# mLSTM heads for four samples at once, with the prompt's final state made in one piece ahead of the samples

## What is computed

```python
def step(carry, inp):                       # one block of frames, b and m are gate sums and running maxima
    C, n, m = carry                         # C: (512 v, 512 k) for each head and stream
    ...
    s = jnp.einsum('bhjd,bhsd->bhjs', qb, kb) * w
    num = jnp.einsum('bhjs,bhsv->bhjv', s, vb) + wp[..., None] * jnp.einsum('bhvd,bhjd->bhjv', C, qb)
    den = jnp.sum(s, axis=-1) + wp * jnp.einsum('bhd,bhjd->bhj', n, qb)
    h = num / jnp.maximum(jnp.abs(den), jnp.exp(-mj))[..., None]
    ...
    C_new = wpL[..., None, None] * C + jnp.einsum('bhs,bhsv,bhsd->bhvd', wsL, vb, kb)
    n_new = wpL[..., None] * n + jnp.einsum('bhs,bhsd->bhd', wsL, kb)
hC = _head_layernorm(hC, norm) + skip * xc  # then x = x + (hC * silu(zg)) @ w_down1
```

## Time and profile before

| | |
|---|---|
| time, median of 3 runs | 2386.26 us (2384.49 to 2390.1) |
| the profiled execution: its time / its span | 2387.82 us / 2386.0 us |
| mean granted TensorE clock | 0.968 of 2.4 GHz |
| TensorE busy / VectorE / ScalarE / GpSimd | 94% / 42% / 20% / 35% |
| bytes moved | 224.24 MB, 94 GB/s over the span |

### The profile page before, as it was taken

One profiled execution on the slowest core, in us unless ns is written; L12 is line 12 of the kernel. 1 busy time (PEld: TensorE's weight loads), 2 busy tenths in 40 slices (PEclk: granted clock), 3 DMA queues, 4 the chain that ended last, 5 costly groups with the idle time before them and its releaser, 6 DMA issues.

```text
span 2386.0 us, 35273 instructions
## 1 busy us (share of the span) xinstructions
PE 2233.5 (94%) x13637; PEld 1985.8 (83%) x13637; DVE 1008.2 (42%) x1342; ACT 474.7 (20%) x695; POOL 845.1 (35%) x492
## 2 busy tenths in 40 slices
PE   6999997899999999999999898998979899999997
PEld 5898996899999998999875564745559899999996
DVE  4565565432220025793236566474642322220025
ACT  4333333211110002221221302213110211100011
POOL 4323321545454545554401000010115454444443
PEclk9999999899999999999999899998989999999998
DMA  4121221212222222322223416062352122222222
GB/s 165 52 89 54 84 87 38 71 62 70 77 73 78 72 77 90 117 79 100 94 87 145 176 48 251 22 229 93 139 198 71 62 71 76 73 75 75 77 73 88
DMA packets 57295, 224.24 MB, mean 94 GB/s; under 512 B 6288, under 2 KB 11280, under 8 KB 48272
## 3 DMA queue, kind: packets, MB, share of 16 engines
q1 hardware_dynamic: 48576, 202.94, 24.1%
q10 hardware_dynamic: 8656, 20.39, 2.3%
HBM read 170.06 MB, written 53.25 MB: 94 GB/s over the span
## 4 chain that ended last, share of the span: by engine, by line
PE 78%; DVE 10%; issue 4%; DMA 3%; ACT 3%; DVEq 1%; POOL 0%; SPq 0%; ACTq 0%; POOLq 0%
PE psd L204 10%; PE psd L208 9%; PE psd L209 9%; PE psd L205 9%; PE psd L211 9%; PE psd L210 9%; PE psm L1217 3%; DMA Cs<-st_c 3%; DVE cv L902 2%; PE psd L1126 2%; PE psm L1188 2%; DVE ntmp L277 2%; PE psm L1224 2%; PE psd L1224 2%; PE psm L382 2%
## 5 line engine op out<-in xcount | busy, mean ns | idle before, releaser
L1722 POOL CAST whi<-wraw 128x1024 fp32r<-128x1024 f32 x224 | 238.7, 1066 | 963.9 <-PE psd L211 504.8
L1724 POOL TENSOR_TENSOR wlo<-wraw,whi 128x1024 fp32r<-128x1024 f32 x224 | 543.4, 2426 | 17.9
L204 PE MATMUL psd<-xh,whi 128*128 128x320 f32 x1280 | 407.3, 318 | 31.7 <-ACT xh L250 19.1
L208 PE MATMUL psd<-xl,whi 128*128 128x320 f32 x1280 | 402.4, 314 | 10.8 <-POOL xl L285 8.7
L205 PE MATMUL psd<-xh,whi 128*128 128x320 f32 x1280 | 399.2, 312 | 0.0
L209 PE MATMUL psd<-xl,whi 128*128 128x320 f32 x1280 | 398.7, 312 | 0.0
L210 PE MATMUL psd<-xh,wlo 128*128 128x320 f32 x1280 | 398.7, 311 | 0.0
L211 PE MATMUL psd<-xh,wlo 128*128 128x320 f32 x1280 | 398.5, 311 | 0.0
L204 PEld LDWEIGHTS psd<-xh,whi 128*128 128x128 f32 x1280 | 243.9, 191 | 35.9 <-issue 29.5
L208 PEld LDWEIGHTS psd<-xl,whi 128*128 128x128 f32 x1280 | 243.1, 190 | 18.9 <-POOL xl L285 13.8
L205 PEld LDWEIGHTS psd<-xh,whi 128*128 128x128 f32 x1280 | 244.0, 191 | 0.8 <-issue 0.2
(11 more groups left out here) (355 smaller groups left out, 3377.1 us busy)
## 6 DMA issues: line engine op xcount, KB each, us to landing
wraw<-w SPq DMA_DIRECT2D x224, 512.0 KB, 3.2
Cs<-st_c SPq DMA_DIRECT2D x32, 1024.0 KB, 6.7
c_s<-Cs SPq DMA_DIRECT2D x32, 1024.0 KB, 4.7
z_kept<-zb ACTq DMA_DIRECT2D x16, 320.0 KB, 2.2
ztp<-z_kept SPq DMA_DIRECT2D x4, 1024.0 KB, 5.4
c_p<-Cp SPq DMA_DIRECT2D x4, 1024.0 KB, 3.9
xT<-x SPq DMA_DIRECT2D x4, 640.0 KB, 6.7
x_kept<-xT ACTq DMA_DIRECT2D x1, 2560.0 KB, 8.6
```

What stands on the lines that cost most here:

```text
L204: pe.matmul(o0, wh, x0, start=st, stop=False)
L208: pe.matmul(o0, wh, l0, start=False, stop=False)
L1722: pool.tensor_copy(whi[s][:], wraw[s][:]).then_inc(w_high, 1)
L1724: pool.tensor_tensor(wlo[s][:], wraw[s][:], whi[s][:].bitcast(F32), ALU.subtract).then_inc(w_split, 1)
```

## The change

- **Samples four at a time.** The loop is over 8 units (o, k): o picks the even or the odd samples, k one feature tile. A unit's `Cs` slot holds the k-tile of four samples, [128, 4, 512] as before, the same 1 MB. `pe_read` reads it by 4 matmuls with a stationary operand of 128x32, each into its own 32 partitions of one bank; `pe_update` makes the update with 4 matmuls of K=32, each on its own 32 partitions of operands and into its own bank. VectorE's four instructions per unit stay (1 per sample instead of 1 per tile). The DRAM side of a transfer now has pieces of 2 KB (one row of 512) instead of 8 KB.
- **The prompt without a running state.** All later chunks take their part straight from scores between chunks ("off": 3 matmuls of 384, 256 and 128 columns for each k); the off-diagonal scores are scaled by ScalarE. The final state is one accumulation of 16 matmuls of 512 columns, for which `ktok` is weighted with products of decays (w2, w3, w4). It stands ahead of the units.
- **The tail goes into the next head.** (c) of head h-1 is cut into pieces (`pe_tail_tok`, `_sum`, `_var`) that stand between the projections of head h; the last head's runs by itself. Gate product and low part move to GpSimd, as do the blocks. The prompt's variance gets the denominator's square times 4 eps added, so that no reciprocal is needed.
- **DMAs.** Loads run on across heads, two units ahead; `z` is loaded at unit 2, once the head before has used its own; the stretch of 4 heads is written out instead of looped.
- **ln_exp_set** loads one table set with Ln and Exp at the norms, at layer 0's gates and head norms and in this mixer; in the whole program 27 table loads are written instead of 48.

```diff
+        def ln_exp_set(a):
+            a.preload_act_table_set("natural_log_exp_and_others")
...
             def act(self, a):
+                ln_exp_set(a)
                 for k in range(KD):
                     a.wait_ge(*self.x_at(k))
...
+            def unit(self, u):
+                return u // KH, u % KH
...
+            def pe_project(self, pe, h, k):
...
+                elif h:
+                    pe.wait_ge(S_.sem, S_.at("rt", h - 1))
+                    pe.wait_ge(V_.sem, V_.at(("C", NB - 1, KH - 1), h - 1))
+                for j in range(2):
+                    pe.matmul(B[j], w[:, j, :], xc[:, ft, 0:SEQ], start=True, stop=True)
+                for j in range(2):
+                    mm = pe.matmul(bank[0][:, tt(j)], w[:, j, :], xc[:, ft, SEQ:T], start=True, stop=True)
...
+            def pe_read(self, pe, h, u):
...
+                pe.wait_ge(self.cin[s], 16 * (n + 1))
+                for j in range(KH):
+                    mm = pe.matmul(B[1][32 * j:32 * (j + 1), :], qz[:, par_, k, 32 * j:32 * (j + 1)], Cs[s][:, j, :],
+                                   start=False, stop=(u == NB - 1), skip_group_check=True)
...
+            def pe_update(self, pe, h, u):
...
+                for j in range(KH):
+                    pe.wait_ge(*((V_.sem, V_.at(("C", u - 1, j), h)) if u else (S_.sem, S_.at(("num", j), h))))
+                    pe.matmul(U[j], ktok[32 * j:32 * (j + 1), NP, tt(k)], vm[par_][32 * j:32 * (j + 1), :], start=True,
+                              stop=True).then_inc(P_.sem, 1)
...
+                for k in range(KH):
+                    pe.wait_ge(V_.sem, V_.at(("qh", k), h))
+                    for c in range(NP - 1):
+                        mm = pe.matmul(off[c], kT[:, k, tt(c)], qT[:, k, P * (c + 1):SEQ], start=(k == 0 and c < 2),
+                                       stop=(k == KH - 1), skip_group_check=True)
...
+                for k in range(KH):
+                    if k >= 2:
+                        pe.wait_ge(S_.sem, S_.at(("Cp", k - 2), h))
+                    for c in range(NP):
+                        mm = pe.matmul(bank[k % 2], ktok[:, c, tt(k)], vtok[:, c, :], start=(c == 0), stop=(c == NP - 1))
...
+                    if u == 6:
+                        pe.wait_ge(self.G.sem, self.G.at("sD", h))
...
+                        for k in range(KH):
+                            for c in range(NP):
+                                pe.matmul(bank[0][:, P + k:P + k + 1], ktok[:, c, tt(k)], ones[:, 0:1], start=(c == 0),
+                                          stop=(c == NP - 1))
...
             def act_head(self, a, h):
...
+                    if h and k == 1:
+                        self.act_d_s(a, h - 1)
+                    if h and k == 2:
+                        self.act_rs_s(a, h - 1)
+                    if h and k == 3:
+                        self.act_hi(a, h - 1)
...
+            def act_d_s(self, a, h):
...
+                a.wait_ge(self.VT.sem, self.VT.at("xcS", h))
+                a.activation(sqs[:], hb[:, KH * h:KH * (h + 1), SEQ:T], ACT.Square).then_inc(self.ST.sem, 1)
...
             def sp(self, sp):
...
+                    for u in range(NB):
+                        n = NB * h + u
+                        store(n)
...
+                        if n >= 1 and n + 2 < NB * H:
+                            load(n + 2)
```

More of the change, by code:

```diff
@@ L801, in trunk @@
         Z_FIRST = 10
[L803 to L806, removed]
         class MLstm:
@@ L1060, in vec @@
                     v.wait_ge(self.zst[s], 16 * CI // 2)
-                with v.Fori(0, H - 1) as h:
-                    self.vec_head(v, h, True)
-                self.vec_head(v, H - 1, False)
+                v.memset(qz[:], 0.0).then_inc(self.qz0, 1)
+                for h in range(H):
+                    self.vec_head(v, h)
+                self.vec_tail(v, H - 1)
             def pe(self, pe):
@@ new lines, in pe_tail_tok, with pe_tail_sum @@
+            def pe_tail_tok(self, pe, h):
+                pe.wait_ge(self.S.sem, self.S.at("rt", h))
+                pe.wait_ge(self.V.sem, self.V.at(("C", NB - 1, KH - 1), h))
+                for f in range(KH):
+                    mm = pe.transpose(bank[1][:, tt(f)], rt[:, f, :], ident)
+                mm.then_inc(self.PT.sem, 1)
+            def pe_tail_sum(self, pe, h):
+                pe.wait_ge(self.ST.sem, self.ST.at("numS", h))
+                for k in range(KH):
+                    mm = pe.matmul(bank[2][:, 0:P], ones, hb[:, KH * h + k, SEQ:T], start=(k == 0), stop=(k == KH - 1))
+                mm.then_inc(self.PT.sem, 1)
@@ L1271, in vec_head @@
-            def vec_head(self, v, h, more):
-                P_, V_, S_ = self.P, self.V, self.S
-                v.wait_ge(P_.sem, P_.rounds(h))
-                v.wait_ge(S_.sem, S_.rounds(h))
-                one = lambda x, i: x[:, bass.ds(i, 1), :].rearrange("p a c -> p (a c)")
-                v.tensor_copy(selh[:], con[0:H, bass.ds(CON["sel"] + P * h, P)]).then_inc(V_.sem, 1)
-                for k in range(KH):
-                    if k < KH - 1:
-                        self.blocks(v, h, k + 1, V_.sem)
+                        pe.matmul(B[0], ones, kT[:, 0, 0:SEQ], start=True, stop=True).then_inc(P_.sem, 1)
@@ L1483, in act_head @@
-                for t in range(2, NP):
-                    num(t)
-                a.activation(att1[:, 0:SEQ], pD[1][:, 0:SEQ], ACT.Abs).then_inc(S_.sem, 1)
-                for b in range(2, 5):
-                    queries(b)
+                a.wait_ge(V_.sem, V_.at(("ex", NP), h))
+                a.activation(att[:, 0:T], att[:, 0:T], ACT.Exp).then_inc(S_.sem, 1)
+                a.wait_ge(P_.sem, P_.at("off", h))
+                a.wait_ge(V_.sem, V_.at("w3", h))
+                scores = (bank[0][:, 0:3 * P], bank[1][:, 0:2 * P], bank[0][:, 3 * P:4 * P])
```

903 lines of the change are left out of this document (455 added, 448 removed).

## The result

The changed kernel takes **2325.1 us** (median of 4 runs, 2323.8 to 2332.2) against 2386.2: ratio 0.9748, 95% interval 0.9725 to 0.9771, faster by 61 us. The forecast was faster, 2284 us, range 2255 to 2318: right in direction, 41 us too low, and outside its range.

The account below looks back on a forecast made before the run. TensorE was taken as busy nearly everywhere, with DMA a close second limit in the samples. The stage's 93.5 us and the tables' 9.0 made 102.5 off 2387.8: 2285.3, as median 2284 us, range 2255 to 2318.

Parts of the forecast that it names:

- (c): The samples' tail of a head, 20.2 us before; forecast gone from heads 0 to 2, its matmuls moved into (a).
- The stage: First projection of head 0 to first down-projection, 4 heads: 566.9 us before, forecast 473.4, 93.5 less.
- Tables: Table loads between Ln and Exp gone: 6.4 us in 5 norms, 2.6 in layer 0's last head norms, 9.0 together.
- The last tail: Last state update to the down-projection, 18.8 us before; forecast 23.
- (a): A head's projections and prompt: 59.8 us before, forecast 60.8 in heads 1 to 3.
- Its new wait: In (a), ScalarE's square of the samples queued ahead of the copies of k for tile 2: 2.8 us.
- (b): A head's samples, eight units after the change: 59.9 us before, forecast 51.7 to 57.9, taken as 55.
- my upper figure of 57.9: Upper end for (b)'s eight units, with TensorE at 1.2 GHz; lower end 51.7, 55 taken.
- a slot's round trip is: Claimed limit in (b) instead of TensorE: 12.5 to 14.2 us from store u to u+2, 6.2 to 7.1 per unit.
- Transfers bind harder: Rival: a load takes 9 us, three loads in a row in (b), 5.7 us a head more: 2307 us; chance 0.22.
- The array's parts don't work at once: Rival: reads and updates 3.4 us each, a round trip of 15.4, (b) at 68: 2336 us; chance 0.04.
- Everything falls well: Rival: TensorE mostly at 2.4 GHz, (b) at 51.7, no stall behind `act_d_s`: 2260 us; chance 0.20.

Follow-up runs that it names:

- e1: Kernel before, with only the Ln and Exp table set loaded ahead in the norms and layer 0's gates and head norms: 2377.2 us.
- e10: Changed kernel with sums behind unit 3, stores from ScalarE's queue, 1 MB of z loaded early, samples' squares behind the third projection's copies: 2282.2 us.
- e7: Changed kernel with matmuls that compute nothing needed behind units 1, 3 and 5, to keep TensorE's clock up: 2320.5 us.
- e6: Changed kernel with each unit's transfers in pieces of 8 KB instead of 2 KB, output not the reference's: 2326.7 us.
- e2: Changed kernel with the 1 MB part of z loaded ahead of a head's first store: 2312.2 us.
- e5: Changed kernel with the samples' state stores issued from ScalarE's queue, leaving SP's queue to the loads: 2294.2 us.
- e4: Changed kernel with the block of sums for the normalisers behind the update of unit 3 instead of unit 6: 2299.9 us.
- e13: e10 with the block of sums behind unit 2 instead of unit 3: 2258.5 us.
- e14: e13 with each load and store cut into two DMAs of two samples (0.5 MB): 2252.2 us.
- e8: Changed kernel with a read's four matmuls on the same 32 output partitions, running one by one, output not the reference's: 2368.9 us.
- e16: Changed kernel with state stores cut to two of a unit's four samples, the other half not written: 2315.7 us.
- e3: Changed kernel with the load of unit n+2 issued ahead of the store of unit n in SP's queue: 2314.5 us.

## Why the prediction was 41 us too low

The stage was to take 473.4 us and took 514.1, 40.7 more. By its own terms:

- **Tables**: 9.0 forecast, 9.6 in the trace, 9.2 alone (e1). Right.
- **The last tail**: 23 forecast, 23.0. Right.
- **(a)**: 60.8 forecast, 62.3 to 62.9 in heads 1 to 3, 54.1 for 52.9 in head 0: 6.6 us in all. Its new wait was forecast at 2.8 and is 3.0 (e10 takes it away). In head 1 the excess lies in the projections, which take 25.3 us up to the scores (1336.12) for 23.2; the rest takes 37.1 for 37.6.
- **(b)**: this is the step that failed. 55 forecast; 63.3, 66.3 and 62.4 in heads 1 to 3, 57.1 for 50 in head 0: 34.1 of the 40.7 us. The path through it was right, the sizes on it were not: the clock, the z loads, the load and the last unit, as taken apart below.

Within (b) the mechanism was right: TensorE stopped being the limit, and the path leads through the loads of units 2, 4 and 6, each with its read, update and VectorE, then the sums and unit 7, as the sum had it. Reads took 1.0 us for 0.86, and the update of four parts 1.07 (from 1374.12 to the read at 1375.19). By the Trainium skill (TensorE: Matmul & The Clock Gate, "Measured speedup vs the span model") the update was estimated at 1.12 us. The trace bears this out better than my 0.86. From read to last state it came to 4.8 us all the same (1373.19 to 1378.00), and to 6.7 at low clock for my 6.6. That is luck: VectorE waits for all four updates, not for the first, and its four instructions take 2.70 us together, not 3.0.

What was mis-sized, in head 1, against my upper figure of 57.9 (everything at 1.2 GHz):

1. "so I expect mostly 1.2 GHz and take the middle": the clock was 0.66 over the stretch, with four of the eight reads and five of the eight updates at half speed, among them all those of the path behind a wait for a load. The upper figure was the one to take, 2.9 us a head; e7 wins 3.1 us a head back in heads 1 to 3. That short bursts between waits for DMAs start at half clock is what the Trainium skill says (same page, "HAM oscillation — how this bites in real kernels"). I had written down that it gives the upper figure, and not followed it; the trace agrees with it at reads 2, 4 and 6.
2. "6.49 x 1.1 = 7.1" for a load: 7.94 and 7.38 us. A load beside its own store alone took 7.3 in this head, near the forecast, though pieces of 8 KB are only 0.4 us faster there (e6). The load of unit 2 has unit 1's store and unit 3's load beside it, which the sum put at nothing: 0.9 us on the first round trip.
3. "1.7 for the z loads": store 2 to store 4 took 18.3 us for the 15.9 that I had with them, 2.4 more. They put 1.7 us of issuing ahead of the load, and share the engines with it too (9.45 us). e2 gets 3.2 us a head back.
4. The last unit "with 4.8": 5.9, since its update is at low clock again behind a read at full clock, 1.1 more. The load of unit 6 took 0.2 more with its issue, its read and update 4.0 for 3.5, the sums 7.2 for 7: together 0.9.

2.9 + 0.9 + 2.4 + 1.1 + 0.9 = 8.2 us, the 63.2 of head 1 less 55. Only head 1 is taken apart; head 2, at 66.3, has 3 us more that are not.

The name given to the limit was wrong too: "a slot's round trip is". With three slots a slot's round trip spans three units, and the sum counted two, because SP issues a load behind the store of two units before. So the number had the order of SP's queue in it, and this is not where the 41 us went; but what the kernel could still gain stayed hidden behind the name. With the same three slots and the same DMAs, a second queue takes off 30.9 us (e5), and the sums at another place 25.2 (e4) and later 23.7 (e13 against e10).

Of the rivals, "Transfers bind harder" (2307) was nearest in time, and half right. It wanted three loads of 9 us on the path; they took 7.9, 9.5 and 7.4 in head 1, so only the one behind z did. The load of unit 5, also behind z, took 11.3, but the path doesn't lead through it. That the engines were not full throughout is shown by e5 and e14, which raise the DMA share from 0.73 to 0.83 and 0.84. "The array's parts don't work at once" falls with e8, "Everything falls well" with the clock. Of the signs named, the reads (1.00 us), the waits for `Cs` and the sums were as forecast; the stores (8.3 us apart on average, 2.7 to 5.1 and 9.5 to 13.3 by turns), the DMA share (0.73, not above 0.8) and TensorE's share (0.57, not below half) were not.

A load's median of 7.9 us comes apart so far: in head 1 a load beside its own store alone takes 7.3, in pieces of 8 KB 6.9 (e6), with half that store 6.2 (e16), and issued ahead of its store 6.2 (e3, all heads' median). The rest goes with the other unit's traffic beside it, which wasn't varied by itself. Open is why such a load takes 8.7 in head 2, and why the kernel before has 6.5 where e6, in the same pieces, has 6.9.

## What to carry to other kernels

When an engine is relieved and the stretch doesn't shrink, look in the chain for queue pieces (here `SPq`) ahead of the transfers: a load that stands behind a store in one in-order queue waits for something it doesn't need, and a second queue can be worth much (whether a fourth buffer would do as well was not tried). A block of work that must be done somewhere is hidden in front of a missing load, up to the length of that wait, and costs its length anywhere on the path; and the place has to be looked for again after every other edit. Gains of edits measured one by one did not add (12.9, 25.2 and 30.9 us gave 33.9), and more came back only when the next obstacles were moved (66.6 us in e13).

## What the runs showed of the hardware

- DRAM traffic in both directions, pieces of 2 KB: 339 GB/s over 12.9 us at a share of 1.00; pieces of 8 KB made the median load no shorter (8.3 against 7.9 us), and one beside its own store alone 0.3 to 0.5 us shorter (e6).
- Of a load and a store issued 0.4 us apart the one issued first lands first and the other pays: 7.9 and 5.2 us with the store ahead, 6.2 and 8.4 with the load ahead (medians of after and e3). Beside its own store alone a load took 7.3 to 8.7 us, with half that store 6.0 to 6.8 (after, e16).
- Four reads of 128x32 on four parts of the array: 1.0 us at full and 1.9 at half clock, on one part 3.6 us at full clock (after, e8). Four updates of 32x128 on four parts: 1.07 us.
- Without the table loads, 1.28 us each, five norms and layer 0's head norms gave 9.2 us together (e1).
